# Decode attention of one transformer step: rotary products in four column groups, the last join on another engine, six weight blocks multiplied earlier

## The reference

```python
def mla_sample(q_nope, q_rope, latent, k_rope, lat_past, kr_past, w_uk, w_uv):
    q_lat = jnp.einsum('bqhd,rhd->bqhr', q_nope, w_uk)
    s_past = (jnp.einsum('bqhr,bkr->bhqk', q_lat, lat_past)
              + jnp.einsum('bqhd,bkd->bhqk', q_rope, kr_past)) * SM_SCALE
    s_new = (jnp.einsum('bqhr,bkr->bhqk', q_lat, latent)
             + jnp.einsum('bqhd,bkd->bhqk', q_rope, k_rope)) * SM_SCALE
    p = softmax(concatenate([s_past, s_new], axis=-1))
    ...

def run_layer(x, c, pos, conv_prefix, attend, lw):
    mod = (jax.nn.silu(c) @ lw['w_ada'] + lw['b_ada'])[:, None, :]
    sh_a, sc_a, g_a, sh_f, sc_f, g_f = jnp.split(mod, 6, axis=-1)
    u = x * (1 + sc_a) + sh_a
    gb, conv_in, qn, qr, lat, kr = project(u, lw['w_in'], ...)
    ...
```

## Time and profile before

| what | us |
|---|---|
| median of 3 runs (1816.36 to 1821.6) | 1817.23 |
| the profiled execution, its own time | 1817.2 |
| its span in the trace | 1815.4 |
| start to the first transposes of the loop (DVE L625) | 79.23 |
| first to last least score (DVE L639) | 94.47 to 345.55 |
| `phase_input` starts (SP L822) | 363.80 |

### The profile page before, as it was taken

The page is one execution under the profiler, slowest core; times in us unless marked ns, Lnnn a source line. Parts: engine busy times, 40 slices in busy tenths (PEclk is TensorE's granted clock), DMA queues, the critical chain, the costliest instruction groups (busy, mean ns, idle before and its releaser), DMA issues.

```text
span 1815.4 us, 32013 instructions
## 1 busy us (share of the span) xinstructions
PE 1603.9 (88%) x13265; PEld 1434.4 (79%) x13265; DVE 892.2 (49%) x1566; ACT 550.9 (30%) x1046; POOL 288.3 (16%) x254
## 2 busy tenths in 40 slices
PE   4689899669999688878699899999999999999993
PEld 2345445359999667767599899999999999999993
DVE  2486577346533476675425762442442442442446
ACT  1144344322311265565433422112112111111143
POOL 3013445212000122222104400000000000000035
PEclk8699999969999899999799999999999999999996
DMA  9579899042211000000242222112112112112112
GB/s 367 226 275 379 333 371 384 5 142 74 55 47 35 21 15 11 5 15 1 69 130 93 82 71 70 35 35 69 35 35 69 35 35 69 35 35 69 58 53 100
DMA packets 116374, 183.58 MB, mean 101 GB/s; under 512 B 16718, under 2 KB 86294, under 8 KB 112172
## 3 DMA queue, kind: packets, MB, share of 16 engines
q1 hardware_dynamic: 107068, 102.04, 17.3%
q0 software_dynamic: 7424, 75.52, 10.3%
q10 hardware_dynamic: 1776, 4.51, 0.7%
HBM read 172.06 MB, written 9.94 MB: 100 GB/s over the span
## 4 chain that ended last, share of the span: by engine, by line
PE 44%; DVE 4%; ACT 2%; issue 1%; DMA 0%; POOL 0%; POOLq 0%; DVEq 0%; ACTq 0%
PE ps L1905 26%; PE ps L1915 14%; PE ps L1955 4%; DVE wf_hl L2174 0%; DVE ln_y L1679 0%; DVE ln_st L1648 0%; DVE ln_st L1688 0%; PE ps L1631 0%; DVE ln_y L1643 0%; DVE ps L2155 0%; ACT ln_y L1671 0%; DVE ps L2154 0%; DMA wo_raw<-in_w_o 0%; PE ps L1895 0%; ACT L2044 0%
## 5 line engine op out<-in xcount | busy, mean ns | idle before, releaser
L1905 PE MATMUL ps<-mix_conv,wf_hl 128*128 128x384 f32 (+1 forms) x1584 | 271.8, 320 | 0.4 <-DVE mix_attn L2168 0.4
L1905 PE MATMUL ps<-mix_attn,wf_hl 128*128 128x384 f32 (+1 forms) x1584 | 271.0, 320 | 0.0
L1915 PE MATMUL ps<-hid,wd_hl 128*128 128x384 f32 (+1 forms) x1584 | 253.8, 321 | 7.3 <-DVE ln_y L1679 5.4
L1915 PEld LDWEIGHTS ps<-hid,wd_hl 128*128 128x128 f32 x1584 | 251.7, 190 | 8.3 <-DVE ln_y L1679 5.9
L1905 PEld LDWEIGHTS ps<-mix_conv,wf_hl 128*128 128x128 f32 x1584 | 253.3, 188 | 0.8 <-issue 0.7
L1905 PEld LDWEIGHTS ps<-mix_attn,wf_hl 128*128 128x128 f32 x1584 | 253.8, 188 | 0.0
L2186 DVE TENSOR_TENSOR h<-ps,gate 128x384 f32<-128x384 f32 (+1 forms) x66 | 34.0, 516 | 303.2 <-PE ps L1905 288.6
L1703 POOL TENSOR_TENSOR ln_y<-ln_y,ln_g 128x1024 f32<-128x1024 f32 (+3 forms) x18 | 42.5, 2361 | 832.5 <-ACT ln_y L1671 832.5
L2197 DVE TENSOR_TENSOR acc<-ps,acc 128x384 f32<-128x384 f32 (+1 forms) x240 | 123.4, 516 | 95.0 <-PE ps L1915 95.0
L625 DVE STREAM_TRANSPOSE rows_T<-ring 128x1024 f32<-128x1024 f32 x128 | 150.4, 1214 | 27.7 <-DMA ring<-in_cache_latent,idx 25.0
L2048 ACT ACTIVATE hid<-h 128x384 fp32r<-128x384 f32 (+1 forms) x66 | 32.4, 491 | 237.9 <-DVE h L2186 237.9
(11 more groups left out here) (333 smaller groups left out, 2503.3 us busy)
## 6 DMA issues: line engine op xcount, KB each, us to landing
ring<-in_w_ada SPq DMA_DIRECT2D x12, 2048.0 KB, 10.8
wf_raw<-in_w_gate SPq DMA_DIRECT2D x22, 512.0 KB, 3.7
wf_raw<-in_w_up SPq DMA_DIRECT2D x22, 512.0 KB, 4.8
wd_raw<-in_w_down SPq DMA_DIRECT2D x22, 512.0 KB, 5.4
wc_raw<-in_w_in SPq DMA_DIRECT2D x24, 256.0 KB, 3.2
x_nat<-in_x_prompt SPq DMA_DIRECT2D x8, 512.0 KB, 3.6
wo_raw<-in_w_o SPq DMA_DIRECT2D x8, 512.0 KB, 4.6
ln_x<-in_x_prompt SPq DMA_DIRECT2D x8, 512.0 KB, 4.3
```

The source lines that it names most:

```text
L1905: last = pe.matmul(ps[:, bank, 0:tn], a, x, start=j == 0, stop=j == 3 * KD - 1)
L1915: last = pe.matmul(ps[:, 4 + q % 4, 0:tn], a, x, start=j == 0, stop=j == 5)
```

## The change

Five edits, all in `phase_sample` and its hand-over:

1. **Rotary products.** Each of the four matmuls of 512 columns in the first column group becomes four of 128 columns, one in each column group (the four groups are added up later anyway).
2. **Six chunks more ahead of the loop.** `FIRST, LATER = 4, 8` becomes `FIRST, EARLY, LATER = 4, 6, 2`: ten chunks are ahead of group 0 in the ring, two are left for the loop. Their `modulate` and `turn_mod` stand between the steps of the new token's chain.
3. **Weights.** `w_nat` and `w_uq` move from ACT's queue to SP's, behind chunk 3.
4. **The last join** goes from POOL to DVE: one product and three multiply-adds in place of seven instructions.
5. **The last store** has a semaphore of its own that outlives the stage. SP does not wait for it at the end of the stage but ahead of reading the scratch (`fetch`).

```diff
-FIRST, LATER = 4, 8
-LOADS = [("chunk", n) for n in range(FIRST)]
+FIRST, EARLY, LATER = 4, 6, 2
+LOADS = [("chunk", n) for n in range(FIRST + EARLY)]
 for _g in range(NGR):
     LOADS.append(("group", _g))
     if _g % 3 == 2 and _g // 3 < LATER:
-        LOADS.append(("chunk", FIRST + _g // 3))
+        LOADS.append(("chunk", FIRST + EARLY + _g // 3))
...
-                    sp.wait_ge(merged, s + 1)
+                    if s == NS - 1:
+                        sp.wait_ge(merged_last, 1)
+                    else:
+                        sp.wait_ge(merged, s + 1)
+                    stored_at = S["last_stored"] if s == NS - 1 else o_free[s % 2]
...
+                    if n == FIRST - 1:
+                        sp.dma_start(w_nat, w_in_nat).then_inc(wn_in, 16)
+                        sp.dma_start(w_uq, io["w_uq"][0].rearrange("(k p) h d -> p k (h d)", p=P)).then_inc(wq_in, 16)
...
-                sp.wait_ge(o_free[1], 64 * (NS // 2 + 1))
+                sp.wait_ge(o_free[1], 64 * (NS // 2))
...
-                join(NS - 1)
...
-                act.dma_start(w_nat, w_in_nat).then_inc(wn_in, 16)
-                act.dma_start(w_uq, io["w_uq"][0].rearrange("(k p) h d -> p k (h d)", p=P)).then_inc(wq_in, 16)
...
                 turn_mod(FIRST - 1)
+                modulate(FIRST)
                 pe.wait_ge(wn_in, 16)
                 pe.wait_ge(dve1, V["uT"])
...
+                turn_mod(FIRST)
                 pe.wait_ge(act1, A["nat_part"])
...
+                modulate(FIRST + 1)
                 pe.wait_ge(dve1, V["cqn"])
...
                     for a in TILES_AT:
                         rows = slice(32 * a, 32 * a + 32)
-                        last = pe.matmul(ps[0:32, a, :], zk[rows, s, :], krT[rows, g % 2].rearrange("p i n -> p (i n)"),
-                                         start=False, stop=True)
+                        k_rope = krT[rows, g % 2].rearrange("p i n -> p (i n)")
+                        for c in range(4):
+                            at = slice(c * P, (c + 1) * P)
+                            last = pe.matmul(ps[32 * c:32 * c + 32, a, at], zk[rows, s, :], k_rope[:, at], start=False, stop=True)
                     last.then_inc(scored, 1)
...
+                final, parts = row_of(NS - 1)[:, 0:KVR + 1], o_all[:, (NS - 1) % 2]
+                step = Order(dve, last_order)
+                dve.wait_ge(e_out, NS)
+                dve.wait_ge(o_out, NGR)
+                step.then(dve.tensor_scalar(final, parts[:, 0], e4[:, (NS - 1) % 2, 0:1], None, ALU.mult))
+                for f in range(1, GPS):
+                    last = dve.scalar_tensor_tensor(final, parts[:, f], e4[:, (NS - 1) % 2, f:f + 1], final, ALU.mult, ALU.add)
...
+                last.then_inc(merged_last, 1)
...
     def fetch(self, eng, io):
+        eng.wait_ge(self.last_stored, 64)
```

More of the change, by code:

```diff
@@ L178, in phase_sample @@
         wk_in = sem("w_uk_in")
-        ada_in = [sem(f"ada_in{j}") for j in range(FIRST)]
+        ada_in = [sem(f"ada_in{j}") for j in range(RING)]
         lat_in = [sem(f"lat_in{j}") for j in range(RING)]
@@ L220, in chunk_at @@
         def chunk_at(t):
-            n = FIRST + (t - 5) // 3
-            return n if t >= 5 and t % 3 == 2 and n < FIRST + LATER else None
+            n = FIRST + EARLY + (t - 5) // 3
+            return n if t >= 5 and t % 3 == 2 and n < FIRST + EARLY + LATER else None
         def mod_row(n):
@@ L234, in store @@
                 def store(s):
-                    sp.wait_ge(merged, s + 1)
+                    if s == NS - 1:
[3 more added lines that the diff above has]
+                    stored_at = S["last_stored"] if s == NS - 1 else o_free[s % 2]
                     for j in range(PARTS):
-                        sp.dma_start(io["o_scratch"][s, j], o_row[32 * j:32 * j + H, s % 2, :]).then_inc(o_free[s % 2], 16)
+                        sp.dma_start(io["o_scratch"][s, j], row_of(s)[32 * j:32 * j + H, :]).then_inc(stored_at, 16)
                 stored = 0
-                for n in range(FIRST + LATER):
-                    while n >= FIRST and 3 * (n - FIRST) + 1 > GPS * stored + 9:
+                for n in range(FIRST + EARLY + LATER):
+                    while n >= FIRST + EARLY and 3 * (n - FIRST - EARLY) + 1 > GPS * stored + 9:
                         store(stored)
                         stored += 1
-                    if n == FIRST:
+                    if n == FIRST + EARLY:
                         sp.wait_ge(dve1, V["kr"])
@@ L316, in row @@
                     act.activation(mod_part[:, n % 2], ps[:, mod_row(n), :], ACT.Copy).then_inc(row_out, 1)
-                for n in range(FIRST):
+                for n in range(FIRST + 1):
                     row(n)
@@ L328, in _ @@
                 act.activation(stat[:, 4:6], stat[:, 2:4], ACT.Sqrt).then_inc(act1, 1)
+                for n in range(FIRST + 1, FIRST + EARLY):
+                    row(n)
                 for t in range(SLOTS):
@@ L472, in score @@
                                 b = 4 * half + c
-                                last = pe.matmul(ps[32 * c:32 * c + 32, a, :], q32[rows, s, b, :], latT[rows, g % 2, :, b, :],
-                                                 start=half == 0, stop=half == 1 and c > 0)
+                                pe.matmul(ps[32 * c:32 * c + 32, a, :], q32[rows, s, b, :], latT[rows, g % 2, :, b, :],
+                                          start=half == 0, stop=False)
                     for a in TILES_AT:
                         rows = slice(32 * a, 32 * a + 32)
-                        last = pe.matmul(ps[0:32, a, :], zk[rows, s, :], krT[rows, g % 2].rearrange("p i n -> p (i n)"),
-                                         start=False, stop=True)
+                        k_rope = krT[rows, g % 2].rearrange("p i n -> p (i n)")
+                        for c in range(4):
+                            at = slice(c * P, (c + 1) * P)
+                            last = pe.matmul(ps[32 * c:32 * c + 32, a, at], zk[rows, s, :], k_rope[:, at], start=False, stop=True)
                     last.then_inc(scored, 1)
```

36 lines of the change are left out of this document (29 added, 7 removed).

## The result

The changed kernel takes 1821.5 us (median of 13 runs, 1812.8 to 1828.0), the kernel before 1816.2 (13 runs, 1814.8 to 1821.6). The ratio is 1.0024, with 1.0013 to 1.0035 as 95% interval: slower by about 0.2%, where 1789 and a gain of 1.6% were forecast. The profiled execution took 1822.2 us, its span is 1820.3.

The account below looks back on a forecast made before the run. PE's instruction list, not the transfers, was taken to set a plain loop slot (7.22 us). Terms: 1817.2 - 18.3 - 14.3 - 6.0 + 18.8 - 8.5 = 1789 us, range 1777 to 1808.

Parts of the forecast that it names:

- Rotary products, -18.3: PE's loop slots: splitting over four column groups cuts 0.86 us to 0.27, 0.59 a slot, 31 slots, -18.3 us.
- the issue rival: Rotary matmuls pass PE one by one, 1.06 us a slot instead of 0.27: +24.5, so 1813 us; chance 0.10.
- The 81 ns of the Trainium skill: Skill's issue gap per 128-column matmul with weight loads: 2.6 us for 32 rotary matmuls, sum 1861; doubted in the prediction.
- Six chunks, -14.3: Loop: six chunks taken out save 2.39 us each of slot time, -14.3 us, called certain.
- stalls, -6.0: Loop: with two chunks in the ring, 2.2 of 8.2 us of stalls remain, -6.0 us, between 0 and -8.2.
- Chain, +18.8 (+15 to +27): New token's chain ahead of the loop: early chunks move the first transposes from 79.23 to 98, +18.8 us.
- a third of the way: Chain: 98 us chosen for its end, between 94.5 and 105.9, the high ends being durations at half clock.
- The weights alone: Chain: loading the first chunks without the two weights gains the projection nothing; its start stays as before, within 2 us.
- The end, -8.5: End of the first stage: 4.5 us instead of 13.0 from the start of the last join, -8.5 us.
- The limit of 358 GB/s: Skill's HBM limit for one core: chunk 9 would land at 96.7, the sum 8.5 higher, 1797; prediction left it to measurement.
- the loop by transfers: Rival: landings set the loop's pace, it keeps 251.1 us, mean slot from 7.77, run 1827.5 us; chance 0.07.

Follow-up runs that it names:

- split_undone: The changed kernel with the rotary products put back in one column group (8 records a slot instead of 32); 1812.2 us, ratio to before 0.997.
- groups_held: The changed kernel, but POOL's first group load waits until chunk 9 has landed; 1803.6 us, ratio to before 0.9925.
- arrival_order: The changed kernel with groups held until chunk 8, projection ahead of chunk 4, five early chunks and two column groups; 1788.1 us, ratio to before 0.9844.
- end_alone: The kernel before with only the last join on DVE and its stores waited for in the next stage's fetch; 1807.9 us, ratio 0.9952.
- no_group_loads: The changed kernel with two small transfers in place of each group's loads from group 6 on, PE's instructions kept; 1796.1 us (one run).
- two_groups: The changed kernel with rotary products in two column groups of 256 columns instead of four of 128; 1810.4 us, ratio to before 0.9944.
- no_early: The changed kernel with its six early chunks back in the loop (eight there, four ahead of the chain); 1827.2 us, ratio to before 1.0057.

## Why the prediction was wrong

The mechanisms of the other steps were right, the chain's with a wrong choice of the clock; one step had the wrong sign and made three quarters of the miss.

- **Rotary products, -18.3: the step that failed.** The working took 0.59 us a slot by 31 slots, with PE still last and nothing else in the way. Undisturbed it is 0.44, so -13.6 would have been the sum. But the same 31 slots with and without the split give 237.1 and 230.7: +6.4. What failed is "nothing else in the way": the sum put the supply of PE's instructions at nothing. I had counted what an instruction costs in PE's array and how fast PE takes one after the other (the issue rival), but not where the instructions come from. The issue rival itself is refuted: it had 1.06 us behind the other scores where 0.42 were measured, and a plain slot of 7.42 where 6.79 were. The 81 ns of the Trainium skill ("TensorE: Matmul & The Clock Gate", Back-to-back issue gap) do not hold for these tiles: 31 records pass in 0.84 us, 27 ns each.
- **Six chunks, -14.3, and stalls, -6.0:** together -20.3. split_undone has this and no split: 251.1 - 230.7 = -20.4. Right as a sum, 3.4 a chunk. The runs do not separate the two terms, but both kinds of stall went: DVE's waits for rows fell from 25.0 us to 3.5, ACT's for POOL's joins from 8.4 to none.
- **Chain, +18.8 (+15 to +27):** +25.1 here, +23 in three runs with the same chain. Right in its cause, which groups_held shows: without groups on the transfers it is 86.8 - 79.2 = +7.6. The landings of chunks 8 and 9 came as forecast (82.8 and 88.2). But chunk 7, at 77.4, was the last that PE waited for; from there its own work set the start, and everything from 75 to 100 ran at half clock (0.50). So "a third of the way" was the choice that failed: 104.3 is near the 105.9 of half clock throughout. The clock fell while PE waited, and in groups_held, without these waits, it was 0.94 from 60 to 75.
- **The weights alone:** right that this buys nothing as long as chunk 4 stands ahead of the projection. arrival_order shows the 9.8 us that lie there.
- **The end, -8.5:** -8.45 in end_alone; -6.8 in the changed kernel, since the last weighing fell to half clock (3.59 instead of 1.93). Join 1.9 for 2.0.
- **The limit of 358 GB/s** in the Trainium skill ("DMA: Bandwidth & Descriptors", Specifications) did not bind: 413 GB/s were moved from 60 to 75 us, and chunk 9 landed at 88.2, not at 96.7.
- **Rivals:** the loop by transfers decided from a mean slot of 7.77; 7.65 looks close, but split_undone has the same transfers and a mean slot of 7.44 (230.7 / 31). None of the rivals named the supply of instructions.

In the first stage the miss is 4.4 + 28.3 = 32.7 us: 24.7 from the rotary products, 6.3 from the chain and 1.7 from the end.

What stays open: why the packets come late. The runs show that it takes both more records and the groups' transfers; no run changes the packets alone. Once a packet moves it is not slow: the 17 that a pause follows took 0.95 us each in the middle, the other 23 of that loop 1.00 and those of no_group_loads 1.02. Whether a packet is asked for too late or waits behind the groups' own packets was not tried.

## What to carry to other kernels

Where a loop is written out in full and its engine issues some 50 instructions in a us, count the instructions as a cost of their own: a split that saves array time can be paid back by the packets that bring it, so try the smallest split first (two column groups kept 0.36 of 0.44 us with a third of the added instructions). Look for idle time by "issue" inside a row of equal instructions, and hold it against the instruction queue. Before loads are moved forward, hold back the transfers that would share the engines with them: the same early chunks cost 25 us with the groups beside them and 7.6 without.

## What the chip showed that I had not expected

- PE's pauses for instructions: 0.7 to 2.1 us each, ended 1.3 to 1.6 us after the packet had landed, in every one of the 17 cases here and of the 9 in before, two_groups and split_undone.
- In two_groups a pause of 1.2 us in PE's work was followed by half the clock: 3.17 us for a weighing of 1.93, 9.70 us for a slot of 6.86. Three such slots cost about 9 us. In the changed kernel none of 17 pauses was followed by it, so what decides stays open.
- Groups on q0 held a transfer on q1 up by over 20 us: the projection waited 24.3 us for its weights in no_early.
